# A hybrid decoder layer on one Trainium2 core: the second pair's depthwise convolution on TensorE in place of VectorE

## The reference, cut to what matters

```python
q, k, v, u, gates = mixer_inputs(...)          # RMSNorm, one projection; u is a GLU
# conv branch: causal depthwise convolution of width 31 over u, 1024 channels
xp = jnp.concatenate([left, u], axis=1)
y = lax.conv_general_dilated(xp, conv_w[:, None, :], window_strides=(1,), padding='VALID',
        dimension_numbers=('NWC', 'WIO', 'NWC'), feature_group_count=CONV_DIM)
y = jax.nn.silu(layer_norm(y + conv_b, ln_g, ln_b)) @ w_conv_proj
# dilated attention in three head groups; then x1 = x + (g0 * conv + g1 * attention) @ w_out
# PEER: per token 8 heads pick 16 of 16384 experts each, whose rows are gathered from DRAM
a = jnp.einsum('td,tkd->tk', hb, u_rows)       # dot of the token with each expert's u row
return jnp.einsum('tk,tkd->td', g * gelu(a), v_rows)
```

## Time and profile before

| what | us |
|---|---|
| three runs: median (lowest to highest) | 2430.39 (2429.74 to 2435.66) |
| the profiled execution: time / span | 2434.64 / 2432.8 |
| PE busy (share of the span) | 1675.2 (69%) |
| DVE busy | 1549.8 (64%) |
| ACT busy | 869.8 (36%) |
| POOL busy | 754.0 (31%) |
| gathers of expert rows, share of the 16 DMA engines | 59.9% |

### The profile page before, as it was taken

One profiled execution on the slowest core, in us unless ns is written; L12 is line 12 of the kernel. 1 busy time (PEld: TensorE's weight loads), 2 busy tenths in 40 slices (PEclk: granted clock), 3 DMA queues, 4 the chain that ended last, 5 costly groups with the idle time before them and its releaser, 6 DMA issues.

```text
span 2432.8 us, 30371 instructions
## 1 busy us (share of the span) xinstructions
PE 1675.2 (69%) x10280; PEld 749.0 (31%) x10280; DVE 1549.8 (64%) x3823; ACT 869.8 (36%) x2357; POOL 754.0 (31%) x714
## 2 busy tenths in 40 slices
PE   7988999998696876768677788986433433434343
PEld 3555554444342333334333333332000000000000
DVE  2466555114468888787886876635567675676674
ACT  2121223201454344444434563434333333333332
POOL 0243100001232433333332333324344443434343
PEclk9998999999798887878796888987555555555555
DMA  4333445737798787889796799999999999999998
GB/s 177 119 102 102 153 143 200 299 139 276 274 390 341 289 354 260 337 291 368 296 374 236 298 364 417 375 407 386 389 401 384 403 391 379 392 398 387 398 380 361
DMA packets 129656, 756.10 MB, mean 311 GB/s; under 512 B 16693, under 2 KB 42413, under 8 KB 49741
## 3 DMA queue, kind: packets, MB, share of 16 engines
q0 software_dynamic: 78336, 570.46, 59.9%
q1 hardware_dynamic: 51164, 183.70, 20.3%
HBM read 734.44 MB, written 20.50 MB: 310 GB/s over the span
## 4 chain that ended last, share of the span: by engine, by line
DMA 20%; DVE 17%; PE 8%; issue 6%; ACT 2%; POOL 0%; DVEq 0%; POOLq 0%; ACTq 0%
DMA ring<-in_expert_uv,pick 20%; DVE ring L1760 5%; PE z L1106 4%; PE acc L1224 3%; DVE yT L1657 1%; DVE cand L1702 1%; DVE e L1703 1%; DVE ti L1665 1%; DVE ti L1668 1%; DVE sco L1666 1%; DVE cand L1700 1%; DVE tv L1667 1%; ACT fold L1385 1%; ACT wgt L1383 1%; DVE tv L1664 1%
## 5 line engine op out<-in xcount | busy, mean ns | idle before, releaser
L1035 POOL DMA_INDIRECT ring<-in_expert_uv,pick x544 | 630.5, 1159 | 1052.3 <-PE acc L1224 977.4
L1760 DVE CUSTOM_DVE_ANT_0 ring<-ring,rep 128x1024 f32<-128x1024 f32 x544 | 660.1, 1224 | 374.3 <-DMA ring<-in_expert_uv,pick 353.6
L1224 PE MATMUL acc<-ring,fold 128*32 128x256 f32 x4352 | 477.6, 528 | 562.9 <-ACT fold L1385 558.3
L1106 PE MATMUL z<-wts,hT 128*128 128x384 f32 (+1 forms) x1408 | 649.2, 599 | 40.5 <-DVE tmp L1804 31.3
L1381 ACT ACTIVATE gel<-dots 128x1 f32<-128x1 f32 x544 | 110.0, 202 | 860.1 <-DVE dots L1760 851.7
L1224 PEld LDWEIGHTS acc<-ring,fold 128*32 128x32 f32 x4352 | 103.6, 127 | 911.7 <-ACT fold L1385 827.3
L1106 PEld LDWEIGHTS z<-wts,hT 128*128 128x128 f32 x1408 | 270.5, 208 | 310.9 <-issue 245.8
L1657 DVE SCALAR_TENSOR_TENSOR yT<-uT,vec,yT 128x256 f32<-128x256 f32 x480 | 213.3, 492 | 4.4
L1106 PE MATMUL z<-wts,yT 128*128 128x512 f32 x384 | 194.6, 641 | 7.3 <-ACT yT L1546 4.2
L1385 ACT ACTIVATE fold<-cst,wgt 128x32 f32<-128x32 f32 x544 | 174.8, 321 | 17.7
L1383 ACT ACTIVATE wgt<-gel,pick 128x1 f32<-128x1 f32 x544 | 160.3, 295 | 17.6
(11 more groups left out here) (204 smaller groups left out, 1639.5 us busy)
## 6 DMA issues: line engine op xcount, KB each, us to landing
wts<-in_w_qkv SPq DMA_DIRECT2D x24, 1536.0 KB
wts<-in_w_glu SPq DMA_DIRECT2D x8, 2048.0 KB
wts<-in_w_gate SPq DMA_DIRECT2D x8, 2048.0 KB
wts<-in_w_wq SPq DMA_DIRECT2D x8, 2048.0 KB
ring<-in_k_cache SPq DMA_DIRECT2D x8, 1536.0 KB, 9.4
ring<-in_v_cache SPq DMA_DIRECT2D x8, 1536.0 KB, 8.0
rep<-x_h SPq DMA_DIRECT2D x68, 128.0 KB
ring<-in_expert_uv,pick POOLq DMA_INDIRECT x544
```

What stands on the lines that cost most here:

```text
L1035: eng.indirect_dma_start(ring[:, i % RING, :], None, a["expert_uv"], bass.IndirectOffsetOnAxis(picks(i, 0).bitcast(U32), 0)).then_inc(row_ ...
L1106: mm = eng.matmul(bank[:, 0:w], of[:, k, :], rows[:, k, :], start=(k == 0), stop=(k == depth - 1))
L1224: mm = eng.matmul(acc[b][SUB * c:SUB * (c + 1), col:col + 256], fold[:, i % 4, :], ring[:, i % RING, D + 256 * c:D + 256 * (c + 1)], start ...
L1760: eng.tensor_tensor_reduce(u, u, rep[:, j, :], 1.0, 0.0, ALU.mult, ALU.add, dots[:, i % 4:i % 4 + 1]).then_inc(dot_ready, 1)
```

## The change

The first pair's convolution stays. For the second pair, c being a block of 256 channels (one GLU unit), m its half of 128, k one of eight groups of 32 channels:

- **W(c, k)** takes the place of U: TensorE multiplies the rows of `ub` by the identity four times, each into its own 32 partitions of a PSUM bank, each copy shifted by one more position, for both tiles; four small matmuls put the last positions of tile 1 in front. ScalarE copies the bank (284 columns) to `shifted`, which lies where `uT` was. Even k use `tpb`, odd k `sbk`.
- **B(c, m)** on VectorE multiplies a 0/1 pattern by the taps: 32 diagonals of 128x32, one for each of 4 channel groups and 8 groups of four taps.
- **C(c, m)** on TensorE: eight rounds of four matmuls, one for each channel group in its own column group, 128 rows being 4 shifts x 32 channels, 256 columns, summed in `ob`.
- **CE(c, m)** on VectorE adds the bias and writes `yT`.
- Tile 1's last 32 rows of u go to DRAM ("uo") and come back ("ul", `load_last_u`); the taps are loaded once in the "late" block of SP. GpSimd's copy of the pad and the waits on it go. G for the second pair waits for W instead of U. PE_COST gets `"W": 0.8, "C": 5.2`, so MARK changes.

```diff
@@ plan
             for t, e in each(p, "glu", c):
                 put(e + 1, ("G", t, c))
-                put(e + 3, ("U", t, c))
-                if t >= NT - 1:
+                if p == 0:
+                    put(e + 3, ("U", t, c))
+                if t >= NT - 1 or t == 1:
                     put(e + 2, ("uo", t, c))
+            if p:
+                for m in range(2):
+                    put(e + 1 + m, ("B", c, m))
+                    put(e + 4 + 2 * m, ("C", c, m))
+                    put(e + 5 + 2 * m, ("CE", c, m))
+                for k in range(GROUPS):
+                    put(e + 2 + k // 2, ("W", c, k))
+                if c < 2:
+                    put(e + 6, ("ul", c + 2))
...
@@ sync
+            def load_last_u(c):
+                if c >= 2:
+                    eng.wait_ge(tp_ready, TB.no["W", c - 2, GROUPS - 2] + 1)
+                    eng.wait_ge(s_ready, SB.no["W", c - 2, GROUPS - 1] + 1)
+                eng.dma_start(last_u[c % 2], sc["uh"][:, 2 * P * c:2 * P * (c + 1)]).then_inc(uh_in[c % 2], 16)
...
+                        if t == 1:
+                            eng.dma_start(sc["uh"][:, 2 * P * c:2 * P * (c + 1)], ub[P - SUB:P, i % 2, :]).then_inc(ub_out[i % 2], 16)
...
@@ tensor
+            def shift(c, k):
+                if k % 2:
+                    bank_free(eng, SB, s_free, ("W", c, k))
+                    bank = sbk[SB.bank(("W", c, k))]
+                else:
+                    turn(("W", c, k))
+                    bank = tpb
...
+                for q in range(QUAD):
+                    to = bank[SUB * q:SUB * (q + 1), :]
+                    eng.matmul(to[:, 0:SUB - 1 - q], last_u[c % 2][:, ch], cst[0:SUB, C_ID + 1 + q:C_ID + SUB], start=True, stop=True)
+                for i, t in enumerate(PAIRS[1]):
+                    for q in range(QUAD):
+                        lo = SUB - 1 - q + P * i
+                        mm = eng.matmul(bank[SUB * q:SUB * (q + 1), lo:lo + P], ub[:, NTH["G", t, c] % 2, ch], ident, start=True, stop=True)
+                mm.then_inc(s_ready if k % 2 else tp_ready, 1)
+
+            def convolve(c, m):
+                bank_free(eng, OB, [o_free, o_free], ("C", c, m))
+                eng.wait_ge(diag_ready, 2 * c + m + 1)
+                eng.wait_ge(tp_free, TB.no["W", c, 4 * m + 2] + 1)
+                freed(eng, SB, s_free, ("W", c, 4 * m + 3))
+                for g in range(GROUPS):
+                    for k in range(QUAD):
+                        mm = eng.matmul(ob[SUB * k:SUB * (k + 1), 0:2 * P], diag[m][:, k, g, :], shifted[:, 4 * m + k, 4 * g:4 * g + 2 * P],
+                                        start=(g == 0), stop=(g == GROUPS - 1))
+                mm.then_inc(o_ready, 1)
...
@@ scalar
+                        if k % 2:
+                            eng.wait_ge(s_ready, SB.no[v] + 1)
+                            eng.activation(shifted[:, k, :], sbk[SB.bank(v)][:, 0:USW], ACT.Copy).then_inc(s_free[READ_BY_A], 1)
+                        else:
+                            turned(v, shifted[:, k, :], tpb[:, 0:USW])
...
@@ vector
+                        signal(eng.tensor_tensor(diag[m].rearrange("p k g c -> p (k g) c"), sel, tap, ALU.mult), diag_ready, 2 * c + m + 1)
...
+                        eng.wait_ge(o_ready, OB.no["C", c, m] + 1)
...
+                        signal(eng.tensor_scalar(yT[:, j, :], ob[:, 0:2 * P], cb[:, j:j + 1], None, ALU.add), conv_v, DC * TAPS + j + 1)
...
-                for p in range(2):
-                    if n in CONV[p]:
-                        conv_upto(p, CONV[p][n])
+                if n in CONV[0]:
+                    conv_upto(0, CONV[0][n])
```

More of the change, by code:

```diff
@@ L189 @@
 RING = 6
+GROUPS = 8
+USW = 2 * P + 28
 LEAD_V, LEAD_A = 2, 2
@@ L545, in conv_shares @@
     out = []
-    for p in range(2):
+    for p in range(1):
         first, last = ENDS["conv", p]
@@ L637, in program @@
         stat = ub
+        diag = [x.rearrange("p (k g c) -> p k g c", k=QUAD, g=GROUPS) for x in (tmp[:, 2 * D:3 * D], qTs[:, 0:D])]
+        last_u = [qTs[0:SUB, D + 2 * P * j:D + 2 * P * (j + 1)] for j in range(2)]
+        shifted = uT[:, :, :].rearrange("p c t -> p (c t)")[:, 0:GROUPS * USW].rearrange("p (k t) -> p k t", k=GROUPS)
         flat = ring[:, :, :].rearrange("p r d -> p (r d)")
@@ L887, in _ @@
                         eng.dma_start(w2, a["norm2_w"].to_broadcast([P, D])).then_inc(late_in, 16)
+                        if p == 0:
+                            eng.dma_start(pt[:, D:D + 2 * P], a["taps"]).then_inc(taps_in, 16)
+                            for j in range(2):
+                                eng.wait_ge(ub_out[j], max(UB_OUT[i] for i, (t, _) in enumerate(GLU) if i % 2 == j and PH_OF[t] == 0))
+                            for c in range(2):
+                                load_last_u(c)
                         eng.dma_start(skT, a["sk_t"]).then_inc(late_in, 16)
@@ L1280, in _ @@
                         spread(v[1])
+                    elif v[0] == "W":
+                        shift(*v[1:])
+                    elif v[0] == "C":
+                        convolve(*v[1:])
                     elif v[0] == "H":
@@ L1429, in _ @@
                         if i >= 2:
-                            eng.wait_ge(tp_ready, TB.no["U", *GLU[i - 2]] + 1)
+                            s = GLU[i - 2]
+                            if s[0] in PAIRS[1]:
+                                eng.wait_ge(tp_ready, TB.no["W", s[1], GROUPS - 2] + 1)
+                                eng.wait_ge(s_ready, SB.no["W", s[1], GROUPS - 1] + 1)
+                            else:
+                                eng.wait_ge(tp_ready, TB.no["U", *s] + 1)
                             if UB_OUT[i - 2]:
@@ L1779, in _ @@
                         place(v[1])
+                    elif v[0] == "B":
+                        c, m = v[1:]
+                        if c == 0:
+                            eng.wait_ge(taps_in, 16)
+                            for t in PAIRS[0][0:2]:
+                                eng.wait_ge(tp_ready, TB.no["MT", t, 1] + 1)
+                        else:
+                            eng.wait_ge(o_ready, OB.no["C", c - 1, m] + 1)
+                        first = GROUPS * c + QUAD * m
+                        sel = cst[:, C_FOLD:C_FOLD + SUB].unsqueeze(1).to_broadcast([P, QUAD * GROUPS, SUB])
+                        tap = pt[:, D + GROUPS * first:D + GROUPS * (first + QUAD)].unsqueeze(2).to_broadcast([P, QUAD * GROUPS, SUB])
+                        signal(eng.tensor_tensor(diag[m].rearrange("p k g c -> p (k g) c"), sel, tap, ALU.mult), diag_ready, 2 * c + m + 1)
+                    elif v[0] == "CE":
+                        c, m = v[1:]
+                        j = 2 * c + m
+                        eng.wait_ge(o_ready, OB.no["C", c, m] + 1)
+                        if j == 0:
+                            eng.wait_ge(z_ready, USE_NO["wq", 1, 3] + 1)
+                        signal(eng.tensor_scalar(yT[:, j, :], ob[:, 0:2 * P], cb[:, j:j + 1], None, ALU.add), conv_v, DC * TAPS + j + 1)
+                        eng.sem_inc(o_free, 1)
                     elif v[0] == "G":
@@ L1971, in laid_out @@
     out["cvec"] = by_partition(np.concatenate(cols, axis=1))
+    w = np.concatenate([np.zeros((1, D), np.float32), x["conv_w"][0]], axis=0).reshape(8, 4, 32, 32)
+    out["taps"] = w.transpose(1, 3, 2, 0).reshape(P, -1)
     state = x["state_conv"][0].transpose(2, 0, 1)
```

51 lines of the change are left out of this document (30 added, 21 removed).

## The result

The changed kernel takes 2366.41 us, the median of four runs (2364.97 to 2368.92); the kernel before, timed again beside them, 2430.94 (2429.74 to 2435.66). The profiled execution took 2364.97 us, its span is 2363.1.

The account below looks back on a forecast made before the run. From 707 to 1436.8 us no engine is full and late hand-overs between engines decide; in the last products expert-row gathers do. +38 + 10 - 22 - 23 - 13 = -10 from 2434.6 gives 2424.6 us, range 2368 to 2453.

Parts of the forecast that it names:

- GLU, +38: 707 to 797.3 us: 15 more steps plus W and C lengthen it to 128 us, +38 (between +28 and +50).
- +48: Both GLU stretches, 707 to 822 us: +38 in the first and +10 in the first eight qkv ticks.
- The convolution in the middle, -30.4: 822 to 1436.8 us: the convolution's chain part leaves VectorE, 11.7 us (29%) in rest of qkv, 18.7 (52%) in gates.
- Thirteen steps at 1.15 us, -15.0: 822 to 1436.8 us: nine and four fewer expert steps, each priced at 1.15 us of chain.
- rival 1: All of the second convolution's VectorE time is on the path, -56 in all: 2374 us; chance 0.17.
- The prediction's own sign for rival 1: The middle, 822 to 1436.8 us, gets over 80 us shorter, where the forecast had some 45.
- The last products, -13: 1436.8 to 1679 us: six fewer expert steps, 15.6 us by bytes or 10 by the chain, taken as -13.
- The tail, 0: Expert steps behind the last products: the tail of 272 steps stays as before.
- Edits with no term: Pad copy, SP's loads and stores (0 to +5), waits for the o bank and for C: put at 0.
- rival 3: 707 to 822 us: ScalarE's 32 copies queue behind waits for dots, 32 us, +22 in all: 2452; chance 0.12.
- rival 2: TensorE paces 822 to 1436.8 us, so VectorE's relief is only idle time, +25: 2455; chance 0.14.
- rival 4: The four column groups do not run side by side, 14 us more for each C: 2530; chance 0.02.

Follow-up runs that it names:

- e2: The kernel before with the changed kernel's list of expert steps, nothing else changed; 2396.86 us, 0.986 of before.
- e10: The kernel before with 13 expert steps taken out of the middle (rest of qkv and gate ticks) and done in the tail; 2417.03 us, 0.995 of before.
- e11: The changed kernel with 8 expert steps moved from middle ticks holding three or two into the GLU ticks; 2369.71 us, 0.975 of before.
- e12: The changed kernel with 8 expert steps moved from middle ticks holding three or two to the tail; 2359.93 us, 0.972 of before.
- e4: The changed kernel with 248 VectorE instructions of the convolution's shape put back, two ticks behind the old places; 2421.00 us, 0.997 of before.
- e9: The changed kernel with the same number of steps per stretch, spread evenly over the middle's ticks; 2378.13 us, 0.979 of before.
- e1: The changed kernel with the expert steps laid in the ticks as in the kernel before; 2419.62 us, 0.996 of before.
- e3: The kernel before without taps 1 to 30 of the second pair's convolution, steps as before; 2385.38 us, 0.983 of before.
- e8: The kernel before with 96 TensorE products of zeros by 256 columns added in the middle; 2435.47 us, 1.003 of before.

## Why the prediction came out too slow

- **GLU, +38: measured +33.5.** C, forecast at 4.6 us, took 3.45 to 3.48 us to the next start in six of its eight places, and 5.17 and 4.84 in the other two, at a granted clock of 0.67 and 0.71 behind waits of 3.6 and 5.0 us. W, forecast at 0.7, took 0.77 where it stood without a wait. The timeline of TensorE in after (start, us, line, operation, records):

```profile
758.28 0.26 PE L1246 MATMUL t<-cst,qTs 32*32 32x31 f32 x8
758.47 0.65 PE L1250 MATMUL t<-cst,ub 128*32 128x128 f32 x16
759.05 0.26 PE L1246 MATMUL s<-cst,qTs 32*32 32x31 f32 x8
...
767.88 3.64 PE L1261 MATMUL o<-uT,tmp 128*32 128x256 f32 x64
771.33 1.05 PE L1292 MATMUL acc<-ring,fold 128*32 128x256 f32 x16
```

  35 steps fell there, at a DMA share of 0.92 and 360 GB/s. TensorE was busy 107.3 us of 123.8, not 117 of 128. For the two stretches together +48 was forecast and +46.5 measured, and that is partly luck: TensorE had 10 us less to do than forecast and idled 16.5 us where 11 were forecast, for another cause (the bank `ob` and not ScalarE's fold, below).
- **The convolution in the middle, -30.4: -37.** Right in kind. About half of VectorE's time was on the path, as its chain showed; the size was short in the rest of qkv (29% forecast, 43% measured), where the chain reached back over only 100 of 428 us.
- **Thirteen steps at 1.15 us, -15.0: -53.** This is the step that failed, and the largest part of the error: 38 of the 60 us by which the span fell more than forecast. (The others are 7 of the convolution, 6 of the last products and 8 of the tail.) The price was taken from three pieces of the chain (dot, accumulation, gather) over the steps of the stretch. That leaves out all that stands in the round because a step stands ahead of it, such as TensorE's scores that came late in the four ticks above. And it is a mean, where the plan thinned out ticks of two and three: the steps that left are worth 3.3 to 4.1 us each (e2, e10, e11, e12). The row for a better bound was there: 187.2 us over 43 steps is 4.35 us, the price if all of the stretch goes by its steps, which as the upper end would have given 13 x 3.2 = 42 us more: 2378, and 2332 with rival 1. The prediction's own sign for rival 1, a middle over 80 us shorter, came true without it: the sum had no rival in which the steps are worth more.
- **The last products, -13: -18.5** for the same kind of steps, 5 by the marks (2.75 us each is the tail's pace, and e2's -19.8 says 4).
- **The tail, 0: -7.7.** It was 757 to 761 us in after, e4, e9 and e11 and 763 to 766 in before, e1, e2, e3 and e8, for one step's difference at most. No run here was made for this; it stays open.
- **Edits with no term.** Waits in the first GLU stretch of after (707.8 to 831.6), beside the earlier trace rows:

```profile
ACT gel L1453 <- DVE dots L1843: 42.2, 28, 5.1
PE o L1274 <- DVEq L1882: 7.3, 3, 3.5
PE acc L1292 <- ACT fold L1457: 3.8, 3, 2.4
PE o L1261 <- DVEq L1882: 3.6, 1, 3.6
PE o L1261 <- DVEq L1810: 1.5, 1, 1.5
PE t L1246 <- ACT uT L1466: 0.3, 1, 0.3
```

  TensorE waited 0.3 us for ScalarE's copies ahead of W, so rival 3 did not happen, though ScalarE itself still waits 42.2 us for dots. But 12.4 of TensorE's 16.5 us of idle time here are waits for the bank `ob`: the expert picks (P, L1274) waited 7.3 us for it behind the eviction of C, and C (L1261) 3.6 us behind the other half's eviction and 1.5 behind the picks. The forecast named this wait without a price, and priced the fold's at 11 us, which took 3.8. The Trainium skill, page "TensorEngine Tiling (Array Packing)", PSUM Bottleneck, warns that after such packing the copies out of PSUM may become the bottleneck. This trace shows them as a cost for `ob`, which VectorE reads, and not for ScalarE's copies of W; they are not the bound of the stretch. The same page of the Trainium skill, Key Properties, has a change of tiling mode drain TensorE. No gap shows it here: the 128x32 records begin 0.07 us ahead of the modelled end of the 32x32 ones (758.47 against 758.28 + 0.26), and so do the next 32x32 ones.
- **The other rivals.** TensorE did not pace the middle (rival 2): its busy share rose from 76 and 74% to 78 and 83% while both stretches shortened. The column groups do run side by side (rival 4): 64 records of 256 columns in 3.45 us. All of the convolution on the path (rival 1) names the nearest time for a wrong reason, as e1 and e3 show.

## What to carry to other kernels

Where a stretch is full on no engine, a price per unit of work need not be the sum of that work's own pieces on the chain, as 1.15 against 4.1 us shows here. Take the stretch's time over its units as a high price to reckon with (not a strict bound: in e11's GLU a step cost 4.0 us where the stretch has 3.5, 123.8 / 35), and look whether the plan puts several units into one slot, for here these cost the most. Read a change of a table of costs as an edit of its own, as large as the one it came with: here 53 of the middle's 91 us came from it. And where one resource moves the same bytes before and after, write down how long it is not full in each stretch, as the most that a change can win there. It points to where a step can be put for little (GLU at a share of 0.73 in e1), but does not price it: at 0.92 it made 8 more steps look like 12 us, and they cost 32 (e11).

## What was not expected of the hardware

Products of zeros raised the granted clock of the rest of qkv from 0.82 to 0.86, and the time of the middle stayed (614.7 and 614.2 us). Four column groups of 128x32 with 256 columns, eight rounds in a row, went at 3.45 us, 0.43 a round, where the accumulation's single round before stands at 0.57 to the next product, both at a granted clock of 1.00.
